# A hybrid decoder layer on one core: token shift split at the projection, and a rearranged RWKV recurrence

## What is computed

```
r = zr + (token_shift(zr) - zr) * mu[0]          # the same for k with mu[1] and v with mu[2]
decay, a, g : from low-rank projections of h and token_shift(h)
kk = k * k_k;  kk = kk / |kk| per head
k  = k * (1 + (a - 1) * k_a)
S  <- S diag(decay) + (S (-kk)) (kk*a)^T + v k^T;   y = S r          # per head, token after token
y  = groupnorm(y) * gn_w + gn_b + sum(r*k*r_k) * v;  out = y * g
```

## Time and profile before

| what | value |
|---|---|
| median of three runs | 3534.33 us |
| profiled execution, its time and its span | 3537.43 us, 3535.6 us |
| TensorE, share of the span | 88% |
| VectorE, ScalarE, GpSimd | 57%, 45%, 25% |
| TensorE's mean granted clock | 0.943 |
| the recurrence | 1264.33 to 1994.66 us |

### The profile page before, as it was taken

How to read it: one execution, slowest core, us unless ns; L and a number is a source line. 1 busy time by engine, 2 the same in 40 slices (tenths; PEclk the granted TensorE clock), 3 DMA queues, 4 the chain that set the end, 5 groups by cost and what they waited for, 6 DMA issues and landing times. The chain is left out here.

```text
span 3535.6 us, 74445 instructions
## 1 busy us (share of the span) xinstructions
PE 3095.4 (88%) x27464; PEld 2514.0 (71%) x27464; DVE 2019.0 (57%) x2951; ACT 1608.7 (45%) x2656; POOL 888.8 (25%) x1065
## 2 busy tenths in 40 slices
PE   7999999988898938888888599569999999995899
PEld 5776878865666637777778488458788787874687
DVE  4333761007777724444444333579889798985555
ACT  3332211006777714333333211048788787874332
POOL 1001330002141266776665100000000000000343
PEclk9999999999999969999999799779999999997899
DMA  5444347434000021222110366526877967773343
GB/s 167 171 172 154 135 169 254 149 121 126 6 16 8 10 105 57 70 73 74 63 63 15 114 220 215 227 78 255 313 300 265 352 263 266 288 268 148 125 145 116
DMA packets 230308, 542.20 MB, mean 153 GB/s; under 512 B 26208, under 2 KB 62176, under 8 KB 221824
## 3 DMA queue, kind: packets, MB, share of 16 engines
q1 hardware_dynamic: 211696, 471.48, 37.4%
q0 software_dynamic: 11552, 41.95, 3.3%
q10 hardware_dynamic: 6768, 24.64, 1.7%
HBM read 408.52 MB, written 129.51 MB: 152 GB/s over the span
## 5 line engine op out<-in xcount | busy, mean ns | idle before, releaser
L559 PE MATMUL p_z<-w_in_part,hn_split 128*128 128x512 f32 x2304 | 536.6, 393 | 8.5 <-DVE w_in_part L388 4.5
L559 PEld LDWEIGHTS p_z<-w_in_part,hn_split 128*128 128x128 f32 x2304 | 433.7, 189 | 99.5 <-issue 4.9
L1670 DVE TENSOR_TENSOR e_w_part<-w_gate_up_sb,e_w_part 128x1024 fp32r<-128x1024 f32 x380 | 452.7, 1223 | 64.2 <-ACT e_w_part L1665 62.6
L1665 ACT CAST e_w_part<-w_gate_up_sb 128x1024 fp32r x380 | 398.0, 1055 | 164.7 <-PE pe_gate L2430 74.5
L2430 PE MATMUL pe_gate<-e_w_part,e_xT 128*128 128x512 f32 x1128 | 288.2, 413 | 29.8 <-DVE e_w_part L1670 29.8
L2442 PE MATMUL pe_y<-e_w_part,e_hT 128*128 128x512 f32 x1128 | 277.0, 401 | 13.5 <-DVE e_w_part L1670 13.5
L2430 PEld LDWEIGHTS pe_gate<-e_w_part,e_xT 128*128 128x128 f32 x1128 | 218.8, 197 | 81.7 <-issue 22.9
L2430 PE MATMUL pe_up<-e_w_part,e_xT 128*128 128x512 f32 x1128 | 271.0, 396 | 0.0
L2442 PEld LDWEIGHTS pe_y<-e_w_part,e_hT 128*128 128x128 f32 x1128 | 210.4, 190 | 61.1 <-DVE e_w_part L1670 13.9
L1670 DVE TENSOR_TENSOR e_w_part<-w_down_sb,e_w_part 128x1024 fp32r<-128x1024 f32 x188 | 218.0, 1222 | 61.6 <-ACT e_w_part L1665 61.5
L2430 PEld LDWEIGHTS pe_up<-e_w_part,e_xT 128*128 128x128 f32 x1128 | 211.9, 188 | 51.3
(11 more groups left out here) (423 smaller groups left out, 5949.8 us busy)
## 6 DMA issues: line engine op xcount, KB each, us to landing
w_gate_up_sb<-in_w_gate_dram SPq DMA_DIRECT2D x32, 2048.0 KB, 13.6
w_gate_up_sb<-in_w_up_dram SPq DMA_DIRECT2D x32, 2048.0 KB, 19.5
w_down_sb<-in_w_down_dram SPq DMA_DIRECT2D x32, 2048.0 KB, 9.4
hn_split<-s_hT SPq DMA_DIRECT2D x48, 1024.0 KB, 5.1
s_y<-e_y ACTq DMA_DIRECT2D x47, 512.0 KB
s_hT<-hn_split SPq DMA_DIRECT2D x16, 1024.0 KB, 6.6
s_y<-d_zeros SPq DMA_DIRECT2D x16, 1024.0 KB, 6.4
s_zr<-z_stage SPq DMA_DIRECT2D x48, 256.0 KB, 2.0
```

What stands on the lines that cost most here:

```text
L559: last = nc.tensor.matmul(bank, hs[m % 3][:, a, k, :].bitcast(F32R), w_part(c, b)[:, k, :].bitcast(F32R), start=(k == 0 and a == b == 0), ...
L1665: return nc.scalar.copy(high, src)
L1670: return nc.vector.tensor_tensor(low, src, high, ALU.subtract)
```

## The change

Three parts.

**Token shift split.** VectorE makes two tiles from a PSUM bank of zr, zk or zv: past = z * mu and now = z - past. past goes to s_zr (read one row earlier), now to a new scratch tensor s_zn. The recurrence only adds the two. VectorE now evacuates zk too. mu comes in by three broadcast loads of 256 KB in the projection; the 768 KB load of mu in the recurrence goes.

```diff
+            def evac_mixed(name, i):
+                now, past = STAGED[(name, i)], STAGED[(name + "_past", i)]
+                bank = pZ[:, Z[(name, i)] % BANKS, :]
+                dve.wait_ge(z_done, Z[(name, i)] + 1)
+                wait_free_stage(dve, (name + "_past", i))
+                nc.vector.tensor_tensor(stage[past % Z_STAGES][:], bank, mixes[name], ALU.mult)
+                wait_free_stage(dve, (name, i))
+                dve.drain()
+                nc.vector.tensor_tensor(stage[now % Z_STAGES][:], bank, stage[past % Z_STAGES][:], ALU.subtract).then_inc(ev_dve, 1)
...
+            sp.dma_start(mu_r[:], t["mu_rkv"][0].partition_broadcast(P)).then_inc(s_mu_r, 16)
...
-                store(("zk", i))
-                store(("zv", i))
+                for name in ("zk", "zk_past", "zv", "zv_past"):
+                    store((name, i))
...
-            for i in range(TILES):
-                evac(("zk", i))
...
-            sp.dma_start(mu[:], t["mu_rkv"].rearrange("m n -> (m n)").partition_broadcast(P)).then_inc(par, 16)
...
-                sp.dma_start(z[s][:], t["zr"][bass.ds(i * P + 1, P), :]).then_inc(z_in[s], 16)
+                sp.dma_start(z[s][:], t["zn"][bass.ds(i * P, P), :]).then_inc(z_in[s], 16)
```

```diff
+            def ahead(i, s, j):
+                r_, k_, v_ = (slice(c * RW, (c + 1) * RW) for c in range(3))
+                pool.wait_ge(z_in[s], ((i + 2) // 2 if isinstance(i, int) else j + 2 - s) * 64 + 64)
+                pool.tensor_tensor(rkv[s][:, k_], rkv[s][:, k_], z[s][:, k_], ALU.add)
+                pool.drain()
+                AHEAD.in_order("kk0")
+                pool.tensor_tensor(kk0[:], rkv[s][:, k_], k_k[:], ALU.mult).then_inc(AHEAD.sem, 1)
+                pool.tensor_tensor(rkv[s][:, r_], rkv[s][:, r_], z[s][:, r_], ALU.add)
+                AHEAD.in_order("rkv")
+                pool.tensor_tensor(rkv[s][:, v_], rkv[s][:, v_], z[s][:, v_], ALU.add).then_inc(AHEAD.sem, 1)
+                pool.drain()
...
-                    pool.tensor_tensor(rkv[n][:], rkv[n][:], z[n][:], ALU.subtract)
-                    pool.drain()
-                    pool.tensor_tensor(rkv[n][:], rkv[n][:], mu[:], ALU.mult)
-                    pool.drain()
-                ev("rkv", mul(rkv[n][:], rkv[n][:], z[n][:], ALU.add))
-                pool.drain()
-                ev("kk0", mul(kk0[:], rkv[n][:, RW:2 * RW], k_k[:]))
...
                 ev("T_init", lambda: pool.tensor_copy(T[n][:], i64[:].unsqueeze(1).broadcast_to([P, HV, CK])))
+                if not isinstance(i, int) or i < TILES - 2:
+                    ahead(i, s, j)
```

```diff
-PE_JOBS = (["cum", "G3a", "G3b", "G1a", "G1b", "Tr0a", "Tr0b", "Wa", "X1a", "X1b", "Wb", "TX1a", "TX1b", "G2a", "G2b",
-            "Tr1a", "Tr1b", "MN0", "MN1", "X2a", "X2b", "RT0", "RT1", "TX2a", "TX2b", "Y0", "S0", "Tr2a", "Tr2b", "X3a", "X3b", "S1",
-            "TX3a", "TX3b", "Ya", "Yb", "Tr3a", "Tr3b", "D", "pc", "X4a", "X4b", "TX4a", "TX4b",
-            "Tr4a", "T0", "Tr4b", "T1", "X5a", "T2", "X5b", "T3", "TX5", "Tr5"])
+PE_JOBS = ["cum", "G3a", "G3b", "G1a", "G1b",
+           "Tr0", "X1a", "X1b", "Wa", "TX1a", "TX1b", "Wb",
+           "Tr1", "X2a", "X2b", "G2a", "G2b", "TX2a", "TX2b", "MN0", "MN1",
+           "Tr2", "X3a", "X3b", "RT0", "RT1", "TX3a", "TX3b", "Y0", "S0",
+           "Tr3", "X4a", "X4b", "S1", "Ya", "Yb", "TX4a", "TX4b", "D", "pc",
+           "Tr4", "X5a", "X5b", "T0", "T1", "TX5a", "TX5b", "T2", "T3", "Tr5"]
+ACT_EV = ["P", "cumsb", "Tr0", "X1a", "X1b", "Wa", "sqk", "Wb", "Tr1", "X2a", "X2b", "Pex", "Tr2", "X3a", "X3b", "Y0",
+          "Tr3", "X4a", "X4b", "D", "sqy", "pc", "vcopy", "Tr4", "X5a", "X5b", "T0", "T1", "T2", "T3", "Tr5"]
+DVE_EV = ["G3a", "G3b", "G1a", "G1b", "TX1a", "TX1b", "kp", "ssk", "G2a", "G2b", "TX2a", "TX2b", "MN0", "MN1", "kkn", "RT0", "RT1", "TX3a", "TX3b",
+          "S0", "S1", "Ya", "Yb", "TX4a", "TX4b", "s1", "yc", "Ah", "Bh", "s2", "TX5a", "TX5b", "bon", "yn"]
...
+                def tr(level):
+                    def make(b):
+                        for p in range(4):
+                            last = nc.tensor.transpose(b[:, p * P:(p + 1) * P], T[s][:, 2 * p:2 * p + 2, :].rearrange("p h n -> p (h n)"), ident[:])
+                        return last
+                    job(f"Tr{level}", make, (DV, "G3b" if level == 0 else f"TX{level}b", 0))
...
+                    r = CHUNKS[AB.index(f)]
+                    each(f"X{level}{f}", range(HV), lambda b, h: nc.tensor.matmul(cols(b[at(h)], h // 2, CK), AR1[s][r, h, 0, :], T[s][r, h, :], start=True, stop=True),
+                         (DV, "G1b" if level == 1 else f"TX{level - 1}b", 0))
...
+                        for h in hs_of(f):
+                            for c, r in enumerate(CHUNKS):
+                                last = nc.tensor.matmul(cols(b[r], h // 2, CK), TP[at(h), h // 2, c, :], X[at(h), c, h // 2, :], start=True, stop=True)
...
+                    job(f"TX{level}{f}", make, (AC, f"X{level}b", 0), (AC, f"Tr{level - 1}", 0))
...
-            steps(pe, step)
+            for i in range(1, TILES - 1):
+                step(i, i % 2, {"main", "tail", "prep"}, None)
```

More of the change, by code:

```diff
@@ L1005 @@
 AB = "ab"
-PE_JOBS = (["cum", "G3a", "G3b", "G1a", "G1b", "Tr0a", "Tr0b", "Wa", "X1a", "X1b", "Wb", "TX1a", "TX1b", "G2a", "G2b",
[3 rows of a table removed]
+PE_JOBS = ["cum", "G3a", "G3b", "G1a", "G1b",
[5 rows of a table added]
 PREP_JOBS = ("cum", "pc", "T0", "T1", "T2", "T3")
 TAIL = ("Wa", "Wb", "MN0", "MN1", "RT0", "RT1", "Y0", "S0", "S1", "Ya", "Yb", "sqy", "s1", "yc", "s2", "yn", "ysum", "rsy", "out")
[L1012 to L1017, removed]
+PREP = PREP_JOBS + ("P", "cumsb", "Pex", "sqk", "vcopy", "kp", "ssk", "kkn", "Ah", "Bh", "bon", "T_init", "rsk", "ex", "b", "Kh", "Rh", "rk", "bv")
+ACT_EV = ["P", "cumsb", "Tr0", "X1a", "X1b", "Wa", "sqk", "Wb", "Tr1", "X2a", "X2b", "Pex", "Tr2", "X3a", "X3b", "Y0",
+          "Tr3", "X4a", "X4b", "D", "sqy", "pc", "vcopy", "Tr4", "X5a", "X5b", "T0", "T1", "T2", "T3", "Tr5"]
+DVE_EV = ["G3a", "G3b", "G1a", "G1b", "TX1a", "TX1b", "kp", "ssk", "G2a", "G2b", "TX2a", "TX2b", "MN0", "MN1", "kkn", "RT0", "RT1", "TX3a", "TX3b",
+          "S0", "S1", "Ya", "Yb", "TX4a", "TX4b", "s1", "yc", "Ah", "Bh", "s2", "TX5a", "TX5b", "bon", "yn"]
+AHEAD_EV = ["kk0", "rkv"]
+POOL_EV = ["rsk", "ex", "b", "Kh", "Rh", "rk", "T_init", "rsy", "bv", "out"]
 MAIN_JOBS = [n for n in PE_JOBS if n not in PREP_JOBS]
@@ L1020, with bank_of, before_in_bank @@
 CHUNKS = (slice(0, CK), slice(CK, 2 * CK))
+def bank_of(name):
+    return MAIN_JOBS.index(name) % BANKS if name in MAIN_JOBS else BANKS + PREP_JOBS.index(name) % 2
+def before_in_bank(name):
+    k = PE_JOBS.index(name)
+    for back, names in ((0, PE_JOBS[:k]), (1, PE_JOBS[k:])):
+        same = [other for other in names if bank_of(other) == bank_of(name)]
+        if same:
+            return same[-1], back
 def phase_rwkv(nc, t, ident):
@@ L1234, in step @@
                 ev("out", mul(yo[:], yo[:], g[n][:]))
-            steps(pool, step)
+            ahead(-2, 0, None)
+            step(-1, 1, {"prep"}, None)
+            step(0, 0, {"main", "prep"}, None)
+            with pool.Fori(0, (TILES - 2) // 2 - 1) as j:
+                step(j * 2 + 1, 1, {"main", "tail", "prep"}, j)
+                step(j * 2 + 2, 0, {"main", "tail", "prep"}, j)
+            step(TILES - 3, 1, {"main", "tail", "prep"}, None)
+            step(TILES - 2, 0, {"main", "tail", "prep"}, None)
+            step(TILES - 1, 1, {"main", "tail"}, None)
+            step(TILES, 0, {"tail"}, None)
         @block.scalar
@@ L1272, in x_ @@
                 def x_(level, f):
[L1273 removed]
+                    evac(f"X{level}{f}", X[:, AB.index(f), :, :], narrow)
                 if "prep" in what:
@@ L1420, in step @@
                                                                 heads(Y0[:])[:, half(f), :], ALU.add), (PE, f"Y{f}"), (AC, "Y0"))
+                for f in AB:
+                    fill_T(f"TX4{f}", 4, f)
                 dve.drain()
@@ L1454, in ready @@
                     for name in names:
-                        ring, size = (MAIN_JOBS, BANKS) if name in MAIN_JOBS else (PREP_JOBS, 2)
-                        k = ring.index(name)
-                        e, other = owner(ring[k - size])
-                        if k >= size or not first:
-                            asked.append((e, other, 0 if k >= size else 1))
+                        last, back = before_in_bank(name)
+                        if not (back and first):
+                            asked.append((*owner(last), back))
                     for e in (AC, DV, PO):
```

145 lines of the change are left out of this document (73 added, 72 removed).

## The result

The changed kernel took 3480.43 us, the median of four runs (3476.3 to 3483.74), against 3535.78 us of the kernel before on the same chip: a ratio of 0.984, 95% interval 0.982 to 0.986. It is 55 us faster; 136 were forecast, and the time lies 30 us above the range. The profiled execution took 3483.74 us (span 3481.9), 53.7 less than that of before.

The account below looks back on a forecast made before the run. TensorE's work and waits were taken to bound each recurrence step. Steps 1 to 14 at -113.8 us, with -9, -5, -7, -2.0 and +1.3 elsewhere, summed to -135.5, giving 3399 us; range 3350 to 3450.

Parts of the forecast that it names:

- pauses inside jobs ... I take 1.1 for all: Recurrence, TensorE: pauses within its jobs would cost 1.1 us a step, part of 3.05 us of waits that stay.
- one in 4.8: TensorE's instruction supply: 7.1 packets needed in a 34.2 us step, one in 4.8 us, against one in 5.1 before.
- A granted clock of 0.97 or more: Sign of a right forecast: TensorE's granted clock in steps 1 to 14 would be 0.97 or more.
- T0 behind Bh ... 0.7: Recurrence: TensorE's T0 would wait 0.7 us a step for VectorE's Bh, since VectorE now fills TX4 first.
- cost nothing: GpSimd's sums made a step ahead would cost nothing; +3 us a step if GpSimd were late by all of them.
- the terms for Tr, the halves, the layouts and the tails: TensorE's busy time a step: Tr -1.7 us, Tr4 and X5 no longer in halves -0.6, new layouts nothing, exposed product ends -1.0.
- X1 behind the masks: Recurrence: TensorE's X1 would still wait 0.9 us a step for the masks.
- TX5 behind X5b: Recurrence, level 5: TensorE's TX5 would wait 0.35 us a step for X5b, lacking other work as cover.
- The loop's price: TensorE's hardware loop: each jump costs 3.3 + 2.2 us, or 2.7 us a step, which goes when written out.
- Supply or order holds the step at 37: Rival, chance 0.23: instruction pauses in denser code, or ScalarE's order, hold the step at 37 us; 3438 us in total.
- Everything hides: Rival, chance 0.09: all waits and new layouts hide, a step takes 31.5 us, TensorE's own job lengths; 3361 us.
- it doesn't do what it says: Rival, chance 0.02: GpSimd or a chain through its sums sets the step at 42 us again; time within a few us.

Follow-up runs that it names:

- e1: The changed kernel with each load of z, rkv, sig and a from step 0 on bringing 8 of 128 rows: 3453.94 us, ratio 0.975.
- e9: e7 with the loads of z, rkv, sig and a from step 0 on bringing 8 of 128 rows: 3428.46 us, ratio 0.967.
- e10: e7 with Wa moved ahead of X1a and Wb ahead of TX1a in TensorE's order: 3423.13 us, ratio 0.966.
- e3: The changed kernel with TensorE's steps 1 to 14 in the hardware loop again: 3512.57 us, ratio 0.992.
- e7: The changed kernel with tile loads spread in time, sums of r and v at the step's start, and Ah and Bh ahead of s1 and yc: 3424.57 us, ratio 0.967.
- e5: The changed kernel with GpSimd's sums of r and v made at the start of the step that uses them: 3452.13 us, ratio 0.975.
- e8: The kernel before with only the split token shift and GpSimd's sums a step ahead; other engines' orders and the loop as before: 3535.49 us, ratio 0.998.

## Why the prediction was wrong

**The step at which it failed** is "pauses inside jobs ... I take 1.1 for all", with "one in 4.8" beside it: it set a mean demand against a mean supply. The mean was even lower (92 packets in 561.81 us, one in 6.1; the row of rows 9, now of after), yet pauses were 4.3 us a step:

```profile
q8 instruction: 92, 1.51, 1.1%
```

What the runs show in its place: the pauses end with the landing of a packet, as said above, so it is the supply of instructions that is short at those places, though not in the mean. e1 and e9 against their bases show 2.0 and 1.1 us a step from the loads; where 2 MB of loads stand ahead of a packet, a pause lasts up to 4.7 us.

The rest I put down to bursts of demand. X has 64 instructions in 0.93 us, so a packet of some 230 lasts 3.3 us where such jobs stand in a row. After a pause the supply is no faster than that. In e9, with small loads, a packet starts at 1471.54 us, lands at 1472.42, TensorE goes on at 1473.89 after a pause of 2.06, and the next packet starts at 1475.33, a cycle of 3.8 us; the shortest such cycle in e9 took 3.3. The new orders, so my reading, put dense jobs next to each other and took out waits in which packets could come early. That this density makes the rest is inferred from what stays in e9 and from e10. The traces support it in part: the 248 instructions of an average packet start within 2.5 us at the densest place of after and within 3.1 at that of before, both faster than that cycle. But stretches of 248 within 3.8 us begin at 13% of the instructions in after and at 22% in before, though in after the pauses themselves break such stretches up. No run changed density alone, and this part stays open.

The Trainium skill, "Runtime: NRT & Kernel Launch", Instruction fetch mechanics, says that TensorE's instructions come in blocks of 16 KiB, that the next is fetched while the current one runs, and that the cost of a boundary is mostly hidden. The packets of 0.02 MB agree; hidden it is not here (4.3 us a step). The Trainium skill, in the same section, also warns that a taken branch breaks the fetching ahead; the loop's jump, 29 us by e3, agrees.

**"A granted clock of 0.97 or more"** failed with it: 0.87, with 0.50 beside the pauses. The mark set for failure ("pauses inside jobs above 2 us a step, a clock below 0.9") was met by both. With loads spread and T0 on time it is 0.96 (e7), so the transpositions, 36 a step in e7 too, don't take the clock.

**"T0 behind Bh ... 0.7"** was 1.9, and **ahead "cost nothing"** is its cause: I asked whether GpSimd was late (it was not), not whether its work would slow VectorE. s1, yc and Ah are together 1.7 us a step longer (172 to 335 ns, 692 to 1579, 685 to 1341), and e5 shows that the sums do it: with those of r and v elsewhere T0's wait is 0.7, the forecast's. The Trainium skill, "SBUF — State Buffer", Who interferes with whom, has the rule: VectorE's instruction with two inputs in SBUF contends with a GpSimd instruction that reads SBUF, while a reduction never does. This trace agrees: yc, Ah, kp and kkn doubled, and the reduction in s1 did not: 0.69 us, beside L1212. It isn't two inputs alone, though: the multiplication in s1 reads one tensor and was slowed too, from 0.17 to as much as 0.66 us.

**The sum of a step.** 34.2 forecast, 40.6 measured. Busy time: 31.2 forecast (34.45 - 3.3), 33.3 measured, +2.1, at a clock of 0.86; in e7, at 0.96, it is 30.6, so the terms for Tr, the halves, the layouts and the tails were together about right; no run shows them one by one. Waits: 3.05 forecast, 7.2 measured: pauses in jobs +3.2, T0 +1.2, X1 behind the masks 0.9 as forecast, TX5 behind X5b not there. Together +6.2 of the 6.4. The loop's price was a little too high: 2.7 us a step in the forecast, 2.0 in the steps of e3 against those of after.

**The other terms.** Most held. Step -1: -8.6 for -9. Step 0: -9.8 for -5; TensorE's busy time fell by 5.9 and its idle time by 3.9, and no run looks into why that is more than forecast. Step 15, from its G3 to the next W: 38.2 (1926.62 to 1964.79) to 34.6, -3.6 for -7, inside -3 to -9. Loads and projection together: the first cum starts 1.8 us earlier, -0.7 forecast. VectorE's multiplication from PSUM took 0.69 us and its second operation 0.69, and both were hidden under TensorE's products. ScalarE's waits for ex, 64.2 us in the earlier trace rows, fell only to 42.1 in place of almost none; no wait of TensorE is traced to it.

```profile
ACT c_Pex L1343 <- POOL c_cum L1229: 42.1, 14, 3.0
```

**The rivals.** "Supply or order holds the step at 37" named the right mechanism with 0.23 and half its size: it had one pause of 0.96 us in the earlier trace rows to go by. Its other branch, ScalarE standing at sqy or Pex with X queued behind, did not come: in the waits after, TensorE has none for ScalarE's X. "Everything hides" and "it doesn't do what it says" are out: e3 against e8, both with the loop, gives 0.6% of the time, some 21 us, to the third part's turning and orders; writing it out gives 29 more; the first two parts by themselves 6 (all by the ratios).

**The best version** of these is e7 or e10, 3.3% faster than before against 1.6% of the change as it stands: their 3425 us lie inside the range that was given for the change.

## What to carry to other kernels

When waits are taken out of an instruction-bound stretch, don't compare the instructions of its mean step alone with what the instruction queue brings: look at its densest few microseconds, and look at which bulk transfers stand ahead of its packets. Spread such transfers over the step. When work moves on GpSimd, look up what VectorE does at its new place: operations with two inputs from SBUF took more than twice their time there.

## What the runs showed of the hardware

- At the pauses in jobs of after, TensorE went on 1.25 to 1.6 us after a packet of instructions had landed, and the next packet started 1.1 us or more after that; the shortest cycle from packet to packet took 3.3 us, in after as in e9. With 2 MB of loads ahead a pause was 4.7 us.
- Every stretch at half clock of after, 25 in 13 steps, stood beside a pause, the shortest 1.45 us, and a pause cost more than its length: busy time was 33.3 us a step at a mean clock of 0.86 and 30.6 at 0.96 (e7).
- VectorE's operations with two inputs in SBUF took 0.69 us with GpSimd idle and up to 1.77 beside its sums of 1.26 us; its reduction took 0.69 in both cases.
- The loop costs TensorE packets as well: 96 in 13 steps with it (e3), 86 without (after).
